# A recurrent layer on one core: inverse levels that multiply only the columns they change, and two kinds of product issued in another order round the array

## The reference, cut to what matters

```python
def step(S, inp):
    w_t, k_t, v_t, kk_t, kka_t = inp[:5]
    S = (S * w_t[:, :, None, :]
         - jnp.einsum('bhij,bhj->bhi', S, kk_t)[..., None] * kka_t[:, :, None, :]
         + v_t[..., None] * k_t[:, :, None, :])
    y = jnp.einsum('bhij,bhj->bhi', S, inp[5]) if emit else None
    return S, y
```

## Time and profile before

| | |
|---|---|
| three runs, median | 3552.69 us |
| profiled execution, its own time | 3556.98 us |
| span of the profiled execution | 3555.2 us |
| TensorE clock granted, mean over the span | 0.929 |
| busy: TensorE, its weight loads, VectorE, ScalarE | 3173.9, 2710.2, 1704.6, 1135.4 us |
| the layer `wkv`: first to last product | 1464 to 2219 us, 755 us |

### The profile page before, as it was taken

How to read it: one execution, slowest core, us unless ns; L and a number is a source line. 1 busy time by engine, 2 the same in 40 slices (tenths; PEclk the granted TensorE clock), 3 DMA queues, 4 the chain that set the end, 5 groups by cost and what they waited for, 6 DMA issues and landing times. The chain is left out here.

```text
span 3555.2 us, 77085 instructions
## 1 busy us (share of the span) xinstructions
PE 3173.9 (89%) x34398; PEld 2710.2 (76%) x34398; DVE 1704.6 (48%) x2698; ACT 1135.4 (32%) x1842; POOL 34.5 (1%) x34
## 2 busy tenths in 40 slices
PE   2967989999995997699999999799998988889998
PEld 2955889999992554588989999678887766578877
DVE  5445455654544001555555553365554445546642
ACT  2414343222221001444444443343223322544421
POOL 0002000000000000100000000000000000000000
PEclk9988979999987998799999999889998977999999
DMA  5220213343311221200000000235541210023322
GB/s 197 95 92 23 95 49 121 128 140 116 112 48 62 78 83 48 82 20 23 23 23 19 23 14 10 98 136 174 175 154 52 75 39 7 13 74 94 94 83 83
DMA packets 89939, 273.53 MB, mean 77 GB/s; under 512 B 9360, under 2 KB 14608, under 8 KB 89488
## 3 DMA queue, kind: packets, MB, share of 16 engines
q1 hardware_dynamic: 85008, 258.17, 21.9%
q10 hardware_dynamic: 4608, 10.49, 0.8%
HBM read 252.11 MB, written 16.52 MB: 76 GB/s over the span
## 5 line engine op out<-in xcount | busy, mean ns | idle before, releaser
L511 DVE TENSOR_TENSOR weights_low<-raw_weights,weights_high 128x1024 fp32r<-128x1024 f32 (+3 forms) x298 | 321.2, 1079 | 757.8 <-ACT weights_high L482 757.4
L482 ACT ACTIVATE weights_high<-raw_weights 128x1024 fp32r<-128x1024 f32 (+3 forms) x298 | 280.1, 941 | 968.4 <-PE psum L335 894.4
L335 PE MATMUL psum<-mlp_in_high,weights_high 128*128 128x512 f32 (+1 forms) x1120 | 373.7, 371 | 16.0 <-DVE mlp_in_low L837 11.0
L335 PE MATMUL psum<-mlp_in_low,weights_high 128*128 128x512 f32 (+1 forms) x1120 | 372.5, 370 | 0.0
L335 PE MATMUL psum<-mlp_in_high,weights_low 128*128 128x512 f32 (+1 forms) x1120 | 372.2, 370 | 0.0
L335 PEld LDWEIGHTS psum<-mlp_in_high,weights_high 128*128 128x128 f32 x1120 | 207.8, 189 | 46.2 <-issue 11.8
L335 PE MATMUL psum<-hidden_high,weights_high 128*128 128x384 f32 (+1 forms) x768 | 232.4, 357 | 0.0
L335 PE MATMUL psum<-hidden_low,weights_high 128*128 128x384 f32 (+1 forms) x768 | 231.5, 356 | 0.0
L335 PE MATMUL psum<-hidden_high,weights_low 128*128 128x384 f32 (+1 forms) x768 | 231.5, 356 | 0.0
L335 PEld LDWEIGHTS psum<-mlp_in_high,weights_low 128*128 128x128 f32 x1120 | 208.0, 189 | 28.0
L335 PEld LDWEIGHTS psum<-mlp_in_low,weights_high 128*128 128x128 f32 x1120 | 208.2, 189 | 27.6
(11 more groups left out here) (429 smaller groups left out, 6324.4 us busy)
## 6 DMA issues: line engine op xcount, KB each, us to landing
mod_space<-in_ada SPq DMA_DIRECT2D x112, 512.0 KB, 3.6
raw_weights<-in_mlp_w SPq DMA_DIRECT2D x96, 512.0 KB, 3.9
raw_weights<-in_w_up SPq DMA_DIRECT2D x44, 512.0 KB, 3.6
raw_weights<-in_mlp_w SPq DMA_DIRECT2D x64, 256.0 KB, 3.0
mod_weights<-in_ada SPq DMA_DIRECT2D x16, 512.0 KB, 3.5
work<-in_ada SPq DMA_DIRECT2D x16, 512.0 KB, 3.5
raw_weights<-in_w_down SPq DMA_DIRECT2D x16, 512.0 KB, 3.4
raw_weights<-in_w_in SPq DMA_DIRECT2D x12, 512.0 KB, 4.4
```

Source lines behind the costliest of these rows:

```text
L335: last = nc.tensor.matmul(out[:, a, :] if wide else out, w[:, cols], x[:, at, t0:t1], start=first, stop=final)
L482: nc.scalar.activation(halves_of(ph, j)[0], raw_of(ph, j), ACT.Copy).then_inc(high.sem, 1)
L511: nc.vector.tensor_tensor(lo, raw_of(ph, j), hi.bitcast(F32), ALU.subtract).then_inc(split.sem, 1)
```

## The change

It has four parts.

1. **Half the columns at the levels.** A level changes only every second run of n columns (and for the transposed inverse every other one). Z at all levels, X and T at all but the first, now stream only those: `moving` picks 32 of 64 columns, in runs of n, and the result lands packed, 32 columns a product. The weights stay 64x64.
2. **Half the elements kept.** VectorE's masked copy of Z and ScalarE's copies of X and T (all but the first level) read the packed 128 x 256 and write them `spread_out` into the tile, in runs of n at a distance of 2n. The masks of the levels are packed in the same way by the host.
3. **Units of a group** are laid out direction first, head second, so copies of M, N and R go `by_head` with one dimension more (the same number of elements), and `wkv_z` gets 64 columns more.
4. **B and Y go round.** The loop over the kinds of product moves outside the loops over `h` and `o`, so each kind is issued in all four quadrants before the next kind follows.

```diff
+HALF = CHUNK // 2
...
         def unit(h, d, j):
-            return slice(((h * 2 + d) * 2 + j) * CHUNK, ((h * 2 + d) * 2 + j + 1) * CHUNK)
+            return slice(((d * 2 + h) * 2 + j) * CHUNK, ((d * 2 + h) * 2 + j + 1) * CHUNK)
+        def parts(level, n, turned=False):
+
+            size = LEVELS[level]
+            late = (n // 4 == 0) == turned
+            return slice(n * CHUNK, (n + 1) * CHUNK), size, int(late)
+
+        def moving(ap, level, n, turned=False):
+
+            u, size, s = parts(level, n, turned)
+            return ap[:, u].rearrange("p (b s n) -> p b s n", s=2, n=size)[:, :, s, :]
+
+        def packed(ap, level, n=None):
+
+            size = LEVELS[level]
+            if n is None:
+                return ap.rearrange("p (d b n) -> p d b n", d=2, n=size)
+            return ap[:, n * HALF:(n + 1) * HALF].rearrange("p (b n) -> p b n", n=size)
...
                                 z = Z[f, level, g % 2, :]
+                                out, half = ps[f, b, u], packed(ps[f, b, :], level, n)
                                 if name == "Z":
-                                    last = nc.tensor.matmul(ps[f, b, u], MX[f, g, u], x[:, u], start=True, stop=True)
+                                    last = nc.tensor.matmul(half, MX[f, g, u], moving(x, level, n), start=True, stop=True)
+                                elif name == "X" and level:
+                                    last = nc.tensor.matmul(half, xt_[:, u], moving(z, level, n), start=True, stop=True)
...
+                                elif level:
+                                    last = nc.tensor.matmul(half, z[:, u], moving(xt_, level, n, True), start=True, stop=True)
...
-                                for h in range(2):
-                                    for o in range(2):
-                                        f, to, c = rows_of(o), rows_of(h), own(t, h)
-                                        nc.tensor.matmul(ps[to, b + o, lane(d, j)], MX[f, i, kx(i, h, d, j)], TOK[f, 2 + d, c],
-                                                         start=True, stop=True)
-                                        out = ps[to, b + o, 4 * CHUNK:][:, lane(d, j)]
-                                        nc.tensor.matmul(out, TOK[f, 2 + d, c], MX[f, i, ux(i, h, d, j)], start=True, stop=False)
-                                        last = nc.tensor.matmul(out, TOK[f, 4 + d, c], TOK[f, 6, c], start=False, stop=True)
+                                for what in range(3):
+                                    for h in range(2):
+                                        for o in range(2):
+                                            f, to, c = rows_of(o), rows_of(h), own(t, h)
+                                            out = ps[to, b + o, 4 * CHUNK:][:, lane(d, j)]
...
                         for t in range(xt):
-                            for h in range(2):
-                                for o in range(2):
...
+                            for d in range(2):
+                                g, j = turn_of(d, t) // 2, turn_of(d, t) % 2
+                                for what in range(2):
+                                    for h in range(2):
+                                        for o in range(2):
...
-                        last = act(MX[:, i % GROUPS, 512:1024], ps[:, b, :], ACT.Copy)
+                        level, g = i // GROUPS, i % GROUPS
+                        if level:
+                            last = act(spread_out(work, g * 1024 + 512, level), packed(ps[:, b, 0:4 * CHUNK], level), ACT.Copy)
+                        else:
+                            last = act(MX[:, g, 512:1024], ps[:, b, :], ACT.Copy)
...
-                        last = nc.vector.copy_predicated(two(Z[:, i // GROUPS, i % GROUPS % 2, :]), level(2 + i // GROUPS),
-                                                         two(ps[:, b, :]))
+                        at = i // GROUPS
+                        last = nc.vector.copy_predicated(spread_out(ZS[:, :], (2 * at + i % GROUPS % 2) * 512, at),
+                                                         packed(LEV[:, 2 + at, :], at), packed(ps[:, b, 0:4 * CHUNK], at))
```

More of the change, by code:

```diff
@@ L1885, in wkv @@
         X1, X1T = sb("wkv_x1", [P, GROUPS, 512]), sb("wkv_x1t", [P, GROUPS, 512])
-        Z = sb("wkv_z", [P, len(LEVELS), 2, 512])
+        ZS = sb("wkv_z", [P, (len(LEVELS) * 16 + 1) * CHUNK])
+        Z = ZS[:, 0:len(LEVELS) * 1024].rearrange("p (l s c) -> p l s c", s=2, c=512)
         GA, GK = sb("wkv_ga", [P, 2, 512]), sb("wkv_gk", [P, 2, 512])
@@ L1907, in unit, with spread_out @@
         def unit(h, d, j):
-            return slice(((h * 2 + d) * 2 + j) * CHUNK, ((h * 2 + d) * 2 + j + 1) * CHUNK)
+            return slice(((d * 2 + h) * 2 + j) * CHUNK, ((d * 2 + h) * 2 + j + 1) * CHUNK)
[11 more added lines that the diff above has]
+            return ap[:, n * HALF:(n + 1) * HALF].rearrange("p (b n) -> p b n", n=size)
+        def spread_out(ap, at, level, turned=False):
+            size = LEVELS[level]
+            first = size if turned else 0
+            step = 4 * CHUNK + (-size if turned else size)
+            return ap[:, at + first:at + first + 2 * step].rearrange("p (d m n) -> p d m n", d=2, n=size)[:, :, 0:4 * CHUNK // size - 1:2, :]
         def lane(d, j):
@@ L2119, in solve @@
                         for t in range(xt):
-                            for h in range(2):
-                                for o in range(2):
[L2122 to L2128, removed]
+                            for d in range(2):
[3 more added lines that the diff above has]
+                                        for o in range(2):
+                                            f, to, u = rows_of(o), rows_of(h), unit(h, d, j)
+                                            out = ps[to, b + o, t * CHUNK:(t + 1) * CHUNK]
+                                            if what == 0:
+                                                nc.tensor.matmul(out, MX[f, g, ux(g, h, d, j)], GA[f, g - 1, u],
+                                                                 start=d == 0, stop=False)
+                                            else:
+                                                last = nc.tensor.matmul(out, TOK[f, 6, own(t, h)], GK[f, g - 1, u],
+                                                                        start=False, stop=d == 1)
                     last.then_inc(ring_done.sem, 1)
@@ L2237, in keep @@
                             eng.wait_ge(x_spilled.sem, x_spilled.base + 16)
-                        last = act(two(MX[:, i, 0:512]), ps[:, b:b + 2, 0:4 * CHUNK], ACT.Copy)
+                        last = act(by_head(MX[:, i, 0:512]), lanes(ps[:, b:b + 2, 0:4 * CHUNK]), ACT.Copy)
                     elif name == "K":
@@ L2241, in keep @@
                     elif name == "X":
[L2242 to L2244 removed]
+                        level, g = i // GROUPS, i % GROUPS
+                        if level:
+                            last = act(spread_out(work, g * 1024 + 512, level), packed(ps[:, b, 0:4 * CHUNK], level), ACT.Copy)
+                        else:
+                            last = act(MX[:, g, 512:1024], ps[:, b, :], ACT.Copy)
+                    elif name == "T":
+                        level, g = i // GROUPS, i % GROUPS
+                        if level:
+                            last = act(spread_out(work, GROUPS * 1024 + g * 512, level, True),
+                                       packed(ps[:, b, 0:4 * CHUNK], level), ACT.Copy)
+                        else:
+                            last = act(XT[:, g, :], ps[:, b, :], ACT.Copy)
                     else:
@@ L2334, in keep @@
                         dve.wait_ge(*by_scalar(k, "M", i))
-                        last = nc.vector.copy_predicated(two(X1T[:, i, :]), level(0), ps[:, b:b + 2, 0:4 * CHUNK])
+                        last = nc.vector.copy_predicated(by_head(X1T[:, i, :]), level(0), lanes(ps[:, b:b + 2, 0:4 * CHUNK]))
                     else:
@@ L3094, in level, with half @@
         return (i // (2 * n) == j // (2 * n)) & (i // n > j // n)
-    both = [(level(1).T, level(1)), (level(1), level(1).T)] + [(level(n), level(n).T) for n in LEVELS]
-    both += [(i < j, i > j), (i <= j, i >= j)]
-    out = np.stack([np.concatenate((d0, d0, d1, d1), axis=1) for d0, d1 in both], axis=1).astype(np.float32)
+    def half(n, late):
+        m = (level(n).T if late else level(n)).reshape(CHUNK, -1, 2, n)[:, :, int(late), :].reshape(CHUNK, HALF)
+        return [m] * 4
+    both = [(level(1).T, level(1)), (level(1), level(1).T), (i < j, i > j), (i <= j, i >= j)]
+    both = [np.concatenate((d0, d0, d1, d1), axis=1) for d0, d1 in both]
+    steps = [np.concatenate(half(n, False) + half(n, True), axis=1) for n in LEVELS]
+    out = np.stack(both[0:2] + steps + both[2:], axis=1).astype(np.float32)
     return np.concatenate([out, out], axis=0)
```

30 lines of the change are left out of this document (20 added, 10 removed).

## The result

| | before | after |
|---|---|---|
| median | 3553.58 us | 3627.89 us (3612.99 to 3636.73) |
| ratio | | 1.0207, interval 1.0175 to 1.0238 |
| profiled execution, its own time and span | 3556.98, 3555.2 us | 3636.73, 3635.0 us |
| mean granted clock over the span | 0.929 | 0.900 |

The change makes the kernel 2.1% slower, 74 us, where 1.2% was forecast. The profiled execution is the slowest of the four. The page of after: TensorE has as many records as before and is busy longer, VectorE and ScalarE are busy less, and the clock row has new low digits in the middle, where the layer stands.

What follows compares the result with a forecast made beforehand. The layer was taken to last as long as TensorE needs for its records. From 3557 us: -49 (B, Y) - 3 (waits) + 98 - 3 (clock) = 3600, less 4 for the median: 3596 us, range 3495 to 3650.

Steps and rivals of the forecast that it cites:

- The case with 48%: Whole kernel: slower by the clock's mechanism, with a clock cost of 65 to 150 us; own range 3560 to 3650 us.
- The clock, 98 - 3 = 95 us: Layer: falls at `sums` and `yvar` cost 98 us over eight passes, less 3 for two falls already there.
- the other 20 steps as well, up to E: First and last pass: clock may stay down up to E, 26.1 us; 20 us taken for each.
- That half-filled steps would not raise the clock: Nine steps behind `sums` and `yvar`: clock stays low until `spread` and `yspread`, 9.7 us a middle pass.
- the clock holds: Rival, solves: half-filled steps may be enough to keep the clock up; 3501 us, chance 27%.
- Half the columns, 0 at full clock: 36 of 42 steps a pass: the weight load sets the pace, so 32 columns instead of 64 gain 0.
- Waits -3 us: TensorE's waits for VectorE's copy of Z: shorter copies take back 3 of 8.3 us.
- no waits for it: Sign in the timeline after: VectorE's copy of Z at some 0.45 us, and TensorE never waiting for it.
- B and Y, 49 us: B and Y in four quadrants run at H's 16.7 ns a record, saving 28.6 and 20.3 us in eight passes.
- rotating B and Y does nothing: Rival: PSUM or the order of loads keeps B and Y at the old pace while the clock falls; 3645 us, 5%.
- half the columns do halve the steps: Rival, steps of the solves: half the columns save 134 us; 3367 us, chance 4%.

Runs made afterwards that it cites:

- wide_sums: The changed kernel, with `sums` and `yvar` streaming 64 columns instead of 2: 3533.8 us, ratio 0.9948.
- full_stream: The changed kernel, with the steps of the solves streaming all 64 columns again and the copies keeping the half they need: 3541.11 us, ratio 0.997.
- full_wide: full_stream with `sums` and `yvar` streaming 64 columns instead of 2: 3539.81 us, ratio 0.9955.
- rot_only: The kernel before, with only the new order of B and Y (part 4): 3546.74 us, ratio 0.9979.
- wide_norot: The changed kernel, with `sums` and `yvar` streaming 64 columns and both B and Y in the old order: 3549.46 us, ratio 0.9984.
- rot_b: The kernel before, with only B in the new order: 3551.71 us, ratio 0.9994.
- y_less: rot_only without the second kind of product in Y, 64 of its 128 records a pass: 3531.29 us, ratio 0.9933.

## Why the prediction was right, and where it was off

**Slower, by the mechanism named: right.** Forecast 3596 us, range to 3650, measured 3628. The case with 48% came: the clock falls at `sums` and `yvar`, steps of 32 columns keep it down, `spread` ends it. wide_sums and full_stream, which each take away one of the two conditions, show the cause. Inside the range the result is with some luck: the forecast's own 3560 to 3650 us leave room for a clock cost of up to 150 us, but none for B and Y to fail.

**The clock, 98 - 3 = 95 us: right in size.** wide_sums takes 94 us off. By the timeline the solves lost 86.3 us, 92 were forecast with the waits. Its parts: the first pass +20.9 and the last +21.1 us, where I took 20 each; the six middle ones +44.3 together, where I had 58 less 3. The middle was high for three reasons: I doubled `spread` and `yspread` (2.3 us more), but the clock is back at the end of `spread`, so that `yspread` runs at full pace; in three of the six the clock was down for 17.1 us and not 20.5; and steps at half clock started 1.71 us apart, 0.77 more than at full clock, not 0.82. In the first pass "the other 20 steps as well, up to E" is what happened.

**That half-filled steps would not raise the clock** I had from attention, where records of 2 and of 512 columns take turns. The rival *the clock holds* has a true part: they do hold it where nothing else disturbs it (a clock of 1.00 for 19.3 us from 1638.70), and that is why 10 products a pass decide over 94 us. But they do not hold it where `sums` and `yvar` stand: there it fell in 8 passes of 8, and with full steps around them in 1 to 5.

**Half the columns, 0 at full clock: right.** Steps at 0.94 us, and wide_sums against full_wide. The wide `sums` repeat the reading of the earlier trace rows in this very place: 62 columns more cost 0.03 us in 12 records, 1.39 us to the next start against 1.36. The Trainium skill ("TensorE: Matmul & The Clock Gate", "What overlaps and what doesn't") says that a load overlaps with matmuls under way only in another row group; load and stream would then add up here, and neither measurement agrees with that.

**Waits -3 us: right.** 8.3 to 5.7 us, and the copy of Z at 495 ns, a little over my 0.45 us. The sign "no waits for it" did not come: at the first level they are what they were.

**B and Y, 49 us: wrong, the term that was mis-sized.** The step was "the change issues B and Y as H is issued, so I take H's pace". The pace was there and better, 14.6 ns against 16.7. But the rows of H and M are bursts of 43 and 32 records, each less than the 127 of one packet. B and Y are 416 records of a pass with H's in between. They gave 7.3 + 10.4 = 17.7 us where they stand, 9 us if all is taken off that M to R, E and H lost again, and on the full time 7 us (rot_only) to 16 (wide_norot to wide_sums). A job of B takes 60.9 / 24 = 2.5 us, not 1.6, and Y 3.5 us a pass, not 2.1. What I took for a pace of the whole job was one of a short burst. The rival *rotating B and Y does nothing*, at 5%, was nearer to the time (3645 us) and to this term, but not for its reason: neither PSUM nor the order of loads holds the pace back, since bursts run at 14.6 ns. The layer got 78 us longer, 35 more than the 43 of my sum. 31 of them are B and Y where they stand, 9 are M to R, E and H, and the solves lost 6 less than forecast: 31 + 9 - 6 = 34.

The old order of B at 29.1 ns was thus already near what the supply gives, 26 to 30 ns, and the queue of instructions in the trace of the kernel before could have told it. The steps of the solves are near it too, at 29 ns a record. They have no such pauses, and at half clock they take 1.71 us instead of 0.94, so it is not the supply that sets their pace now; but for the rival *half the columns do halve the steps* the supply would have been in the way as well.

**Open.** Why packets come no closer than 3.3 us: there is no kernel here with the same products in fewer instructions. That the pauses are waits for packets rests on their times, on the debt that moves from B to Y in rot_b, and on y_less; no run changed the supply alone. What B's order alone is worth is open too.

## What to carry to other kernels

Where weights are loaded for every product, fewer moving columns save nothing as long as the load sets the pace, and here they kept a clock low that full streams brought back. Look at what stands behind each place where the granted clock falls; more columns under the loads of the jobs that make it fall cost almost nothing here and cured it. The version that beats both kernels is wide_sums (3533.8 us, 0.5% under before). A pace read from a burst of 30 or 40 records does not hold for 400: compare it with the rate at which instructions arrive over the whole stretch.

## What was not expected of the hardware

- Half-filled steps (32 columns under each load of 64) can stay at either level of the clock: 19.3 us at 1.00, and 54.6 us at 0.50 in the first pass, up to E, at 0.95 and 1.71 us a step. Around the 2-column products the clock fell in 7 and 8 passes of 8 with them, against 1 to 5 with full steps.
- Products that go round four quadrants start 14.6 ns apart, but over some hundred of them TensorE gets a record every 26 to 30 ns; it pauses in between, and every such pause of the layer ends 1.19 to 1.58 us after a 16 KB packet of instructions has landed, with packets never under 3.3 us apart.
- Those pauses can cost twice: in the profile after, three falls of the clock (at 1679.5, 1781.9 and 2085.7, 17.1 us together) come in or right behind a Y with pauses, where the kernel before has none. Rot_only has one fall of 3.4 us in B.
